# A two-block transformer kernel on one core: where its stores are issued, how the last down-projection is grouped, when its sums of squares come, and which table set ScalarE loads

## What is computed

```python
def conv_ffn(h, w_up, conv_w, conv_b, w_down):
    up = h @ w_up
    s_len = up.shape[1]
    padded = jnp.pad(up, ((0, 0), (CONV_WIDTH_2 - 1, 0), (0, 0)))
    conv = conv_b + padded[:, 0:s_len] * conv_w[0]
    for j in range(1, CONV_WIDTH_2):
        conv = conv + padded[:, j:j + s_len] * conv_w[j]
    gate, val = jnp.split(conv, 2, axis=-1)
    return (jax.nn.silu(gate) * val) @ w_down

def second_block(...):
    for l in range(DEPTH):
        h = rms_norm(x, norm1_g[l])
        proj = h @ w_in[l]
        za, xb, q, k, v, g = jnp.split(proj, splits, axis=-1)
        ya = spatial_gating(jax.nn.gelu(za), a_vnorm_g[l], a_ws[l], a_bs[l])
        yb = multiscale_pool(xb, b_w[l], b_scale[l])
        yc = retention(q, k, v, g, c_norm_g[l])
        x = x + jnp.concatenate([ya, yb, yc], axis=-1) @ w_out[l]
        x = x + conv_ffn(rms_norm(x, norm2_g[l]), w_up[l], conv_w[l], conv_b[l], w_down[l])
    return rms_norm(x, final_g)
```

## Time and profile before

| | us |
|---|---|
| median of 3 runs | 4418.41 |
| fastest, slowest | 4415.34, 4421.36 |
| the profiled execution | 4409.52 |
| its span | 4407.7 |
| busy PE | 3960.8 (90%) |
| busy DVE | 2155.2 (49%) |
| busy POOL | 1393.9 (32%) |
| busy ACT | 1098.7 (25%) |
| mean granted clock of PE | 0.956 |

### The profile page before, as it was taken

How to read it: one execution, slowest core, us unless ns; L and a number is a source line. 1 busy time by engine, 2 the same in 40 slices (tenths; PEclk the granted TensorE clock), 3 DMA queues, 4 the chain that set the end, 5 groups by cost and what they waited for, 6 DMA issues and landing times.

```text
span 4407.7 us, 47585 instructions
## 1 busy us (share of the span) xinstructions
PE 3960.8 (90%) x18476; PEld 3120.2 (71%) x18476; DVE 2155.2 (49%) x2838; ACT 1098.7 (25%) x2057; POOL 1393.9 (32%) x924
## 2 busy tenths in 40 slices
PE   5979999799399997889989999998889899999997
PEld 2657778677267776667767888886677677888885
DVE  3755650846656445642336445444442246444545
ACT  3114552122145422322222111111213222111112
POOL 1121001344110123552335333333543254333333
PEclk9989999999699998999989999999899899999998
DMA  4310000033000001420122111111310031111112
GB/s 171 136 70 20 11 1 26 20 102 119 10 20 11 21 6 63 146 69 29 34 79 84 48 48 39 48 46 50 115 53 29 24 116 55 53 51 48 43 50 70
DMA packets 83952, 245.97 MB, mean 56 GB/s; under 512 B 8720, under 2 KB 15888, under 8 KB 82960
## 3 DMA queue, kind: packets, MB, share of 16 engines
q1 hardware_dynamic: 83728, 242.93, 16.6%
HBM read 226.12 MB, written 16.78 MB: 55 GB/s over the span
## 4 chain that ended last, share of the span: by engine, by line
PE 73%; DVE 19%; ACT 4%; issue 2%; DMA 1%; POOL 1%; DVEq 0%; SPq 0%; ACTq 0%; POOLq 0%
PE bank L590 19%; PE bank L591 19%; PE bank L592 19%; DVE wk L1675 4%; PE bank L712 2%; DVE nt L1582 1%; PE bank L698 1%; DVE gw L1810 1%; DVE gw L1799 1%; PE bank L689 1%; PE bank L687 1%; DVE wk L1732 1%; DVE nt L1571 1%; PE bank L562 1%; PE bank L564 1%
## 5 line engine op out<-in xcount | busy, mean ns | idle before, releaser
L590 PE MATMUL bank<-h_hi,w_hi 128*128 128x512 f32 (+1 forms) x3504 | 1381.9, 394 | 43.2 <-POOLq L2119 26.2
L591 PE MATMUL bank<-h_lo,w_hi 128*128 128x512 f32 (+1 forms) x3504 | 1359.7, 388 | 0.0
L592 PE MATMUL bank<-h_hi,w_lo 128*128 128x512 f32 (+1 forms) x3504 | 1358.9, 388 | 0.0
L2117 POOL CAST w_hi<-raw 128x1024 fp32r<-128x1024 f32 (+2 forms) x386 | 389.7, 1010 | 2239.2 <-PE bank L592 1718.5
L2118 POOL TENSOR_TENSOR w_lo<-raw,w_hi 128x1024 fp32r<-128x1024 f32 (+2 forms) x386 | 839.4, 2175 | 30.9
L590 PEld LDWEIGHTS bank<-h_hi,w_hi 128*128 128x128 f32 x3504 | 667.0, 190 | 202.2 <-POOLq L2119 30.9
L591 PEld LDWEIGHTS bank<-h_lo,w_hi 128*128 128x128 f32 x3504 | 666.4, 190 | 151.2 <-issue 10.0
L592 PEld LDWEIGHTS bank<-h_hi,w_lo 128*128 128x128 f32 x3504 | 665.6, 190 | 144.5
L590 PE MATMUL bank<-g_hi,w_hi 128*128 128x512 f32 x704 | 282.2, 401 | 39.6 <-DVEq L2082 26.6
L1327 ACT ACTIVATE wk<-bank 128x512 f32<-128x512 f32 x200 | 119.1, 596 | 791.4 <-PE bank L592 770.4
L2067 DVE TENSOR_SCALAR wk<-wk,v 128x1024 f32<-128x1024 f32 x88 | 89.0, 1011 | 456.5 <-ACTq L1519 438.3
(11 more groups left out here) (247 smaller groups left out, 4797.7 us busy)
## 6 DMA issues: line engine op xcount, KB each, us to landing
raw<-w_in SPq DMA_DIRECT2D x114, 512.0 KB, 3.5
raw<-w_ffn SPq DMA_DIRECT2D x96, 512.0 KB, 3.5
raw<-w_out SPq DMA_DIRECT2D x64, 512.0 KB, 3.7
x<-w_mod SPq DMA_DIRECT2D x16, 1024.0 KB, 4.8
raw<-w_down SPq DMA_DIRECT2D x64, 256.0 KB, 2.6
wk<-residual SPq DMA_DIRECT2D x48, 256.0 KB, 2.6
raw<-w_down SPq DMA_DIRECT2D x48, 192.0 KB, 2.3
gw<-w_mod SPq DMA_DIRECT2D x4, 2048.0 KB, 21.2
```

The costliest lines, as they stand in the source:

```text
L590: mm(o, wh[:, ws], hi[:, at_, t0:t0 + n], start=kt == 0, stop=False)
L591: mm(o, wh[:, ws], lo[:, at_, t0:t0 + n], start=False, stop=False)
L592: last = mm(o, wl[:, ws], hi[:, at_, t0:t0 + n], start=False, stop=kt == nk - 1)
L2117: link(G.tensor_copy(w_hi[:, sl], raw[:, sl]))
```

## The change

1. `GROUPS` ends with (16, 18), (18, 22) instead of (16, 19), (19, 22); group 4 (two rows) is issued after f = 21 and the last one (four rows) after it. `NG` becomes 6, and the two conv buffers `ff_c` move into the norm's buffer `nt`. The first eight adds of group 4 stand between the conv operations of f = 21.
2. The five stores and the load of constants are issued by ACT instead of SP; the load of the rotation table at "bv" of layer 1 waits for the first store.
3. `mean_square(2, 1)` moves from row 2 to row 7 of sv0, `mean_square(3, 1)` from behind i = 3 to behind i = 5, `mean_square(5, 1)` from row 2 of sv0 to behind sv1; ACT's rounding of pass 1 is interleaved otherwise with its gates.
4. `log_and_exp()` loads one table set ahead of each pair of Ln and Exp (norms, conv branch, GLA, retention).
5. In the FFN, ACT copies out the first chunk pair of up tile 4 at f = 1 instead of f = 2.
6. DVE makes the windows of the pooled branch's second half behind the scaling of the gating (`pool_windows(1)` behind L1939).

```diff
-GROUPS = [(0, 4), (4, 8), (8, 12), (12, 16), (16, 19), (19, 22)]
-NG = 5
-
-AFTER = {min(f1, NF - 1): g for g, (f0, f1) in enumerate(GROUPS)}
+GROUPS = [(0, 4), (4, 8), (8, 12), (12, 16), (16, 18), (18, 22)]
+LAST = len(GROUPS) - 1
+NG = 6
+
+
+AFTER = {4: 0, 8: 1, 12: 2, 16: 3, 21: 4}
...
-    ff_c = [a.take(S) for _ in range(2)]
+    assert a.at <= n2
+    ff_c = [nt[:, i * S:(i + 1) * S] for i in range(2)]
...
+                        if l:
+                            sp.wait_ge(sem["store0"], 16)
                         sp.dma_start(at_cs, rope1).then_inc(sem["rope_in"], 16)
...
-                        if l and (p, d) == (1, 6):
-                            sp.wait_ge(sem["t_ready0"], 24)
-                            sp.dma_start(scratch[1][:, :, 0:512], x2[:, :, 0:512]).then_inc(sem["store1_0"], 16)
-                            sp.dma_start(cst2, const[:, NC1:NC1 + 2048]).then_inc(sem["m_tables"], 16)
-                load_through(INDEX[("out1", l, 7, 1)] + 2)
-                if l == 0:
-                    sp.wait_ge(sem["res_ready"], RES0["out1", 0] + 16)
-                    sp.dma_start(scratch[0], x[:, :, 0:S]).then_inc(sem["store0"], 16)
...
-                if l == 0:
-                    g = INDEX[("down", 0, (len(GROUPS) - 1, 7), 0)]
-                    load_through(g + 1)
-                    sp.wait_ge(sem["res_ready"], RES0["down", 0] + 8)
-                    sp.dma_start(scratch[2][:, :, 0:512], x2[:, :, 0:512]).then_inc(sem["store2_0"], 16)
-                    load_through(g + 8 + 2)
...
                     project_as_ready(in2_index(l, IN2[0], p), h2_hi, h2_lo, "h_ready", h_count(n1, p),
-                                     None if p else (5, 1) if l else (2, 1))
+                                     None if p or l else (2, 1), 7)
                     for i in ORDER2[0][1:] if p == 0 else ORDER2[1][1:5]:
                         project(in2_index(l, IN2[i], p), h2_hi, h2_lo)
-                        if (l, p, i) == (0, 0, 3):
+                        if (l, p, i) == (0, 0, 5):
                             mean_square(3, 1)
+                        if (l, p, i) == (1, 0, 1):
+                            mean_square(5, 1)
...
+                        for d in range(DT):
+                            project(INDEX["down", l, (g, d), 0], g_hi, g_lo, f0)
+                pe.wait_ge(sem["g_ready"], NF * l + NF)
+                for p in range(2):
+                    for d in range(DT):
+                        project(INDEX["down", l, (LAST, d), p], g_hi, g_lo, GROUPS[LAST][0])
+                        if (p, d) == (1, 1):
+                            mean_square(5 + 2 * l, 0)
...
+            def log_and_exp():
+
+                nc.scalar.preload_act_table_set("natural_log_exp_and_others")
...
+            def store_half(i, p):
+
+                act.dma_start(scratch[i][:, :, p * 512:p * 512 + 512], x2[:, :, p * 512:p * 512 + 512])\
+                   .then_inc(sem[f"store{i}_{p}"], 16)
+
             def rs_of(n, p):
 
                 _, _, rs, _ = norm_buffers(n, p)
+                log_and_exp()
                 act.wait_ge(sem[f"ms_sum{p}"], n + 1)
...
                     act.wait_ge(sem["re_var"], m + 1)
                     if m:
                         act.wait_ge(sem["re_mixed"], m)
+                    log_and_exp()
                     link(A(re_rs, psum[6][:, :], ACT.Ln, bias=EPS))
...
+                    if f > SKEWF // 2:
+                        up(2 * f, 0)
                     if f >= SKEWF // 2:
-                        up(2 * f, 0)
                         up(2 * f + 1, 0)
                         act.sem_inc(sem["ff_up_ready"], 1)
+                    elif f == SKEWF // 2 - 1:
+                        up(SKEWF, 0)
...
+                    if l == 0:
+                        store_half(2, p)
...
+                pool_windows(0)
                 dve.wait_ge(sem["sg_col_ready"], l + 1)
                 link(V.reciprocal(sg_col, sg_col))
...
+                pool_windows(1)
...
-                    adds = iter([(d, ci) for d in range(DT) for ci in range(2)] if f in AFTER and f < NF - 1 else [])
+                    adds = iter([(d, ci) for d in range(DT) for ci in range(2)] if f in AFTER else [])
...
-                        add_down(d, p, 0)
+                        add_down(LAST, d, p, 0)
```

More of the change, by code:

```diff
@@ L90, in stream @@
                 g = AFTER[f]
-                last = g == len(GROUPS) - 1
-                for p in range(2 if last else 1):
-                    for d in range(DT):
-                        seq.append(("down", l, (g, d), GROUPS[g][1] - GROUPS[g][0], PASS_LAT[p] if last else CH_LAT, p))
+                for d in range(DT):
+                    seq.append(("down", l, (g, d), GROUPS[g][1] - GROUPS[g][0], CH_LAT, 0))
+        for p in range(2):
+            for d in range(DT):
+                seq.append(("down", l, (LAST, d), GROUPS[LAST][1] - GROUPS[LAST][0], PASS_LAT[p], p))
     return seq
@@ L537, in _ @@
                 for j in range(DT):
-                    load_through(INDEX[("down", 1, (len(GROUPS) - 1, 7), 1)])
+                    load_through(INDEX[("down", 1, (LAST, 7), 1)])
                     sp.wait_ge(sem[f"t_ready{p}"], 56 + j + 1)
@@ L566, in row_tile, with project_as_ready @@
                         last.then_inc(sem["acc_ready"], 1)
-            def project_as_ready(g, hi, lo, ready, before, sums=None):
+            def project_as_ready(g, hi, lo, ready, before, sums=None, row=2):
                 for kt in range(SEQ[g][3]):
                     row_tile(g, kt, hi, lo, ready, before)
-                    if kt == 2 and sums is not None:
+                    if kt == row and sums is not None:
                         mean_square(*sums)
@@ L1023, in _ @@
                         pe.wait_ge(sem["g_ready"], NF * l + f1)
-                        for p in range(2 if f == NF - 1 else 1):
-                            for d in range(DT):
-                                project(INDEX["down", l, (g, d), p], g_hi, g_lo, f0)
-                                if (p, d) == (1, 1):
-                                    mean_square(5 + 2 * l, 0)
+                        for d in range(DT):
+                            project(INDEX["down", l, (g, d), 0], g_hi, g_lo, f0)
+                pe.wait_ge(sem["g_ready"], NF * l + NF)
+                for p in range(2):
+                    for d in range(DT):
+                        project(INDEX["down", l, (LAST, d), p], g_hi, g_lo, GROUPS[LAST][0])
+                        if (p, d) == (1, 1):
+                            mean_square(5 + 2 * l, 0)
             mean_square(7, 1)
@@ L1316, in _ @@
                             square(3, 0, j, x2)
+                        if d == 1:
+                            store_half(1, 0)
                     if l and d >= 4:
@@ L1918, in _, with pool_windows @@
                 link(last)
-                for j in range(2):
+                def pool_windows(j):
                     dve.wait_ge(sem["po_in"], 2 * l + j + 1)
@@ L2048, in _, with add_down @@
                         dve.wait_ge(sem["ff_hi"], n)
-                    def add_down(d, p, ci):
-                        g = INDEX["down", l, (AFTER[f], d), p]
+                    def add_down(g, d, p, ci):
+                        g = INDEX["down", l, (g, d), p]
                         q, (t0, w) = FIRST_CHUNK[g] + ci, SEQ[g][4][ci]
@@ L2212, in _ @@
                     split_through(in2_index(l, f"k{j + 1}") if j < 3 else INDEX["out2", l, 1, 0])
-                split_through(INDEX["down", l, (len(GROUPS) - 1, 7), 1])
+                split_through(INDEX["down", l, (LAST, 7), 1])
 _NAMES = ["xT", "cT", "w_mod", "w_in1", "w_out1", "vec1", "vec2", "vec3", "sinks", "gla_up",
```

34 lines of the change are left out of this document (18 added, 16 removed).

## The result

The changed kernel took 4321.55 us (median of 4 runs, 4320.1 to 4324.64) against 4419.68 (4415.34 to 4421.36): ratio 0.9785, 95% interval 0.9773 to 0.9797. The two medians alone give 0.9778; the ratio is that of the means, with the profiled execution of before, 4409.52, among them. Run again later beside another nine runs of the kernel before, it took 4320.06, ratio 0.9779 (0.9766 to 0.9793). So it is 2.2% faster, some 96 us. The forecast was 4331.5 in a range of 4304 to 4370.

What follows compares the result with a forecast made beforehand. PE's matmul stream was taken as the bound, with losses at seams as waits and half clock behind them. Seven terms summed to 86.9 us, taking the median from 4418.4 to 4331.5; range 4304 to 4370.

Steps and rivals of the forecast that it cites:

- FFN end, layer 0: End of FFN layer 0: 45.4 us lost; group 4 as cover, moved store and shorter tail leave 21; gain 24.4.
- FFN end, layer 1: End of FFN layer 1: 22.4 us lost; 4.5 for adds and 3.8 of tail stay; gain 15.4, 14.2 taken.
- FFN starts: PE's 5.29 us wait for ACT's copy of up tile 4 and 3.0 of clock go; 16.6 over two layers.
- Spatial gating: PE's waits for DVE's L1939, 13.3 us in two layers, go, with 1.5 of clock per layer; 16.2.
- Table loads outside the retention: One set spares Exp's load: eight exposed loads at norms, conv branch, GLA and in1, 10.4 us; up norms 1.6.
- The 36.81: PE's idle us in in1 of layer 1, waiting for DVE's conv; an earlier weight tile was to give nothing.
- In the retention (16 pairs) I take 0.: Retention, 16 Ln and Exp pairs: the one load is exposed in place of the Exp load; gain 0 us.
- The third rival: Retention: where `re_var` comes before ACT is free, 4 to 12 of 16 pairs gain; 10 us, 4321; chance 0.1.
- in2 of layer 0: Waits behind the store (2.79) and at `mean_square(3, 1)` (5.12) go, 12.3 with clock; new waits leave net 3.5 us.
- the second rival: Moved stores collide with weight tiles on the DMA engines: 15 us less won, 4347; chance 0.14.
- The first rival: DVE becomes the bound at FFN ends and in2: 36 us less won, gain 51, time 4368; chance 0.12.
- The fourth: PE's clock falls to half in FFN stretches now run without pause; 4456 with 250 us of it; chance 0.03.

Runs made afterwards that it cites:

- the two runs: Changed kernel without hand-placed table loads anywhere, 4344.93 us (26 slower), and without them in the retention alone, 4333.92 us (14 slower).
- store_late: Changed kernel with ACT storing the first half of scratch[1] after block 1's last square instead of after norm 3's first-half squares; 4313.04 us, ratio 0.9761.

## Why the prediction was right, and where not

**The bound** was read rightly: nothing changed inside the FFN stretches, and all that was won was won at seams, part idle time and part clock behind it. Idle time fell by 67.9 us, busy time by 16.9. By stages, forecast and then measured:

- **FFN end, layer 0** (24.4 forecast, 23.1 in the trace). Interleaved adds: 3.3 idle and 1.2 of clock forecast; 3.2 idle and no clock measured, for behind these waits, at most 1.06 us, the granted clock stayed 1.00. Tail: 12.5 idle and 3 of clock forecast, 9.3 and 3.6 measured. The store: the 8.65 went but for 1.12, as forecast.
- **FFN end, layer 1** (14.2): 13.8.
- **FFN starts** (16.6, and 1.6 for the up norms): 15.6 in the trace for both. Tile 4 alone gives 16.1 by the trace of its run and 17 by the times, so its term was right. The 1.6 for the up norms did not come: PE's waits at their rows were 0.55 us in both layers and are 0.65 and 0.63.
- **Spatial gating** (16.2; its own terms, 13.3 and twice 1.5, make 16.3): 13.4 in the trace, 15 by its run. The forecast gave DVE 15 us until PE's next need, the pooled branch (L906); PE now waits 1.12 us there in each layer. Layer 1 gave 5.4 against 8.0 in layer 0 because PE's next wait, for the split of a weight tile behind the rotation table, rose there from 4.72 to 6.01.
- **Table loads outside the retention** (12.0, and 1.3 at the end): 26 - 14 = 12 by the two runs, with the uncertainty of both. The trace alone had 3.3 for block 1, where 10.4 were forecast. There the idle time of PE fell by 10.6, as forecast (single waits by 1.28 each: 11.94 to 10.65 at the conv branch, 10.83 to 9.54 and 8.72 to 7.45 at out1), but PE's busy time in block 1 was 7.3 us longer, with the same matmuls. That is clock: from 263 us to the end of the wait at 293 PE was busy 11.16 us at 0.69 in the execution before, 13.35 at 0.61 after.
- **The 36.81** behind DVE's conv stayed, to the hundredth, as forecast: the weight tile that no longer waits there (4.73 idle) gave nothing.

**The step that failed first: "In the retention (16 pairs) I take 0."** It measured 14 us (16.8 in the trace). The row at 2221.09 is from the last head group, where ACT waits for PE. In the second pair of the others both loads were exposed and PE waited 2.23 us behind them. One row was taken for sixteen. The third rival (chance 0.1) was right, and its price of 10 us was still low. So was the rule that was weighed against the row: the Trainium skill, "ScalarE: Activation LUTs", section "Table sets: the hidden batching unit", counts one load for Ln then Exp, and the trace agrees, with one L1036 ahead of both. The run with one load a head group goes beyond a pair: the set stays through ACT's Square and Copy in between. That the third rival's time, 4321, is also the measured one is chance: stages below their forecast made up for its low price.

**The step that failed second: in2 of layer 0, "net 3.5".** The stage lost 1.2. The failed term is the store's: "the 2.79 behind the store" was to go with 1.7 of clock and the 2.39 ahead of it to stay as it was, and in place of both PE waits 6.46. The forecast took the store off SP's queue and did not ask when ACT would issue it. It went out 13 us earlier than before, into the loads of two weight tiles and two residual tiles. There the second rival (collision on the DMA engines, chance 0.14) held, though only there, at a price of 9 us by `store_late`. The argument against it, "DMA share is 0.32 in the window", was a mean over 87.5 us; while a store is under way the share is 0.92 to 0.96. The Trainium skill, "DMA: Bandwidth & Descriptors", section "Issuing engines are not separate DMA queues", says that transfers of all issuers interleave on the same engines; POOL's 13.12 us agree. Its other half, that a second issuer saves issue time alone, agrees for the transfer too: a 256 KB tile took 7.7 us beside the store on the same queue and 6.3 on the other. PE's 8.49 against 1.12 at the end of the FFN comes from what stands ahead of the transfers in the queue: the store's wait for DVE, which held SP's loads 4.9 us. The terms of the sums themselves were near: 5.12 and 2.7 of clock won less 7 and 1.8 paid is -1.0, and the waits at the rows of pass 1 are 6.2 (1.31, 2.74 and 2.16); the run that moves the sums back has -2.

**The first rival** (DVE takes the bound; gain 51) did not come: PE waited 3.2 us for the eight interleaved adds, where no lead at all would have cost 11.7. **The fourth** (half clock in the FFN) did not come: 1.00 over 605 us.

That the sum came out so near is in part luck. Between the two profiled executions 86.9 us were forecast and 84.9 measured, but the retention was 16.8 over its forecast and everything else together 18.9 under it: block 1 7.1, in2 4.7, gating 2.8, FFN starts 2.6, FFN ends 1.7. Nor are the 9.9 us between 4331.5 and 4321.6 the retention's: the profiled execution of before was 8.9 under its median, which the forecast carried over to the changed kernel, while that of the changed kernel was 3.1 over its own.

## What to carry to other kernels

An operation that occurs sixteen times has to be read in its group and in several places before one instance is taken for its price; the first question is whether the engine was waiting ahead of it. A transfer moved to another engine's queue frees what stood behind its wait, and changes its moment: look at what loads are due in the 10 us after the new moment, and put it where the splitter is ahead. A DMA share taken over a long window says nothing of the share while one large transfer runs. Work that fills a wait could here be interleaved with the chain that PE waited for at the price of 3.2 us of stalls and no clock, for 13.3 covered.

## What the runs showed of the hardware

A 2 MB store issued on ACT's queue delayed a 512 KB load issued 1.1 us later on SP's queue to 9.3 us, against a median of 3.8 us for such loads (w_out). A 256 KB load took 7.7 us when issued 0.6 us behind the store on its own queue, and 6.3 us when issued 2.2 us behind it on the other, against 2.6: a second queue gave no priority. While a store ran, the DMA engines were 0.92 to 0.96 busy with 332 to 334 GB/s.

Five waits of PE of 0.12 to 1.06 us, all within 10 us, left the granted clock at 1.00 (2.4 GHz). Behind a wait of 2.2 us the next four matmuls took 3.0 to 3.7 us at four of six places and 1.96 at two; behind one of 0.96 they took 1.96 at all six. A wait of 5.29 us was followed by 6.80 us at 0.50, 1.2 GHz. Two profiled executions of the same changed kernel, with 379.0 and 379.1 us of idle time on PE, differed by 6.4 us in span.

One load of the table set served Ln, Exp, Square and Copy for two pairs in a row.
